# Gate-and-up products of the gated FFNs: weights stationary instead of tokens in 10 of 11 groups

## Chip, cores and metric

One core of a Trainium2 chip runs the whole program in one launch. The metric is device time in microseconds (us), the median of several executions.

## What is computed

256 tokens of width 1024 pass through two blocks in fp32: two layers with two gated FFNs each (around a short convolution in the first, a gated delta rule in the second), then a block with sparse attention, an RWKV-7 mixer and a convolutional FFN. The change concerns the four gated FFNs, with D_FF = 2816:

```python
def swiglu(x, w_gate_up, w_down):
    gate, up = jnp.split(x @ w_gate_up, 2, axis=-1)
    return (jax.nn.silu(gate) * up) @ w_down

for i in range(DEPTH):
    g = norm_g[i]
    ff = swiglu(rms_norm(h, g[0]), ffn_w_gate_up[i, 0], ffn_w_down[i, 0])
    h = h + 0.5 * rms_norm(ff, g[1])
    ...
    ff = swiglu(rms_norm(h, g[4]), ffn_w_gate_up[i, 1], ffn_w_down[i, 1])
    h = h + 0.5 * rms_norm(ff, g[5])
```

## The kernel before

All weights are streamed once from memory, in *groups* of up to 512 output columns, cut in *tiles* of two k-rows (2 x 128 input channels x 512 columns, 256 KB). A gate-and-up group holds 256 gate columns and the 256 up columns that belong to them, with 8 k-rows: four tiles (the very first group has five). An FFN has 11 such groups, then a down product of two groups with 22 k-rows each.

To come near fp32 with the fast fp32r products, each operand is split in a high part (rounded to fp32r) and a low part (the rest). ScalarE writes the high part of a weight tile (`high_to`, L423), VectorE the low part over the raw tile (`low_to`, L433). Both run up to AHEAD = 5 tiles past the last tile of the group in work (`stream_act`, `stream_dve`). There are 6 high buffers and 10 raw ones, so the high part of tile t waits until TensorE has used tile t - 6, the load of tile t for tile t - 10. The tokens' halves are xh and xl, channels on partitions.

TensorE works group by group (`products`, `tile_products`). Tokens are the stationary operand: for each k-row and each of the two token blocks (TB, 128 tokens each) three products of 512 moving weight columns (L458 high by xh, L459 low by xh, L460 high by xl) add up in one PSUM bank per token block. Groups alternate between bank pairs acc0 and acc1. So the output has tokens on partitions: ScalarE takes silu of the gate half, scaled per token by prs (the norm's factor; L700), VectorE multiplies it with the up half and prs (L706) into prod. The down product needs the inner channels on partitions, so TensorE turns prod with four 128x128 transposes into a bank tr (`transpose_prod`, L716), behind the next group's products. ScalarE writes the high part hh (`hidden_high`, L723), VectorE the low part hl (`hidden_low`, L729).

The order on each engine is what `Ffn.pe`, `Ffn.act`, `Ffn.dve` and `Ffn.pool` write down. Banks tr0 and tr1 are handed out in turn as *units*, with the counters tr_ready and tr_free (`free_unit`). `rest_of_vec_pe` and `rest_of_vec_act` (L3715, L3719) turn the other per-channel vectors once, in the first FFN, behind group 0, into the banks aux.

Of the kernel before, what the change touches and what calls it, by code (L numbers as in the profile page):

```python
# [15 lines left out]
ALU = mybir.AluOpType  # L16
# [169 lines left out]
def build(nc, ins, out, stages):  # L186
# [34 lines left out]
    with ctx:  # L221
# [15 lines left out]
        xh = sb("xh", [P, DC, SEQ], F32R)  # L237
        xl = sb("xl", [P, DC, SEQ], F32R)
# [27 lines left out]
        prs = sb("prs", [P, TB])  # L266

# [15 lines left out]
        acc = [[ctx.enter_context(nc.psum_tensor(f"acc{i}{t}", [P, GW], F32)) for t in range(TB)] for i in range(2)]  # L283
        banks = acc[0] + acc[1]
        tr = [ctx.enter_context(nc.psum_tensor(f"tr{i}", [P, GW], F32)) for i in range(2)]
        aux = [ctx.enter_context(nc.psum_tensor(f"aux{i}", [P, GW], F32)) for i in range(2)]
# [7 lines left out]
        acc_free = [sem(f"acc_free{i}") for i in range(2 * TB)]  # L294
# [26 lines left out]
        stored = sem("stored")  # L321

# [18 lines left out]

        place, earlier, count = [], [], [0] * 4
        for gi, g in enumerate(groups):
            if g[0] == "gdn_vz":
# [3 lines left out]
            elif g[0] == "gdn_out":  # L351

                place.append([2 * (gi - first["gdn_out"]) + t for t in range(TB)])
            else:
                low_pair = gi == 0 or 2 in place[-1] or 3 in place[-1]
                place.append([0, 1] if low_pair else [2, 3])
            earlier.append([count[b] for b in place[gi]])
            for b in place[gi]:
                count[b] += 1

# [10 lines left out]
        plan = dict(unit=0, pre=0, post=0, sil=0, hhc=0)  # L371
# [71 lines left out]
        def tile_products(pe, t, tb, xa, xb, before=None):  # L443
# [5 lines left out]
            if k0 == 0 and earlier[gi][tb]:  # L449
                pe.wait_ge(left(gi, tb), earlier[gi][tb])  # L450
            o = at_acc(gi, tb)[:, 0:n]
# [14 lines left out]
        def products(pe, gi, xa, xb, before=None, at_=None, then=None, at2=None, then2=None):  # L466

            for i, t in enumerate(tiles_of[gi]):
# [4 lines left out]
                for tb in range(TB):  # L473
                    tile_products(pe, t, tb, xa, xb, before)

# [131 lines left out]
        def branch_add(dve, s, tb):  # L607
            if s.norm is not None:
                dve.wait_ge(post_sq[tb], 2 * s.norm + 2)
                nc.vector.tensor_scalar(msq[:, tb:tb + 1], ssq[:, tb, 1:2], ssq[:, tb, 0:1], EPS / s.factor ** 2,  # L610
# [108 lines left out]

        def hidden_high(act, g, u):  # L720
# [12 lines left out]
        class Ffn:  # L733
# [3 lines left out]
            def __init__(self, name, g0, vector):  # L737
# [5 lines left out]
                self.unit = plan["unit"] + DC // 2  # L743
                plan["pre"] += 1
                plan["post"] += 1
                plan["unit"] += DC // 2 + FG
                plan["sil"] += 2 * FG
                plan["hhc"] += FG
# [3 lines left out]

            def pe(self, pe, nxt):
                first_products(pe, self)
                if self.n == 0:
                    rest_of_vec_pe(pe)
                for g in range(1, FG):
                    products(pe, self.up + g, xh, xl)
                    transpose_prod(pe, self.up + g - 1, self.unit + g - 1)

                def before(k, tb):
                    u = self.unit + k // 2
# [3106 lines left out]
```

## Time and profile before

| | us |
|---|---|
| median of 3 runs | 1620.4 |
| lowest, highest | 1620.27, 1620.67 |
| span of the profiled execution | 1619.2 |

The span is from the first to the last instruction of the one execution that was profiled; that execution has no time of its own beside it, so it is set against the median of the runs. In the profile, PE is TensorE's matmul, PEld its weight load, DVE VectorE, ACT ScalarE, POOL GpSimd. Durations of matmuls are of pipelined instructions and overlap: the rate is read from their starts.

### The profile page before, as it was taken

What the parts mean: (1) busy time and instruction counts of PE and PEld (TensorE: products, weight loads), DVE (VectorE), ACT (ScalarE), POOL (GpSimd) and SP (SyncE); (2) the same over time, 40 slices, a digit from 0 to 9 for tenths busy, and PEclk for the clock granted to TensorE, in tenths of its full rate; (3) what the DMA queues carried; (4) which work ended last, traced back from release to release, by engine and by line L of the source; (5) the groups of instructions that cost most, each with busy time, mean ns of one, the idle gap of its engine ahead of it and who ended that gap; (6) DMA issues with size and microseconds to landing.
All of it is one profiled execution on the core that took longest, in us unless ns stands there. A gap on an engine that the chain in (4) does not pass through costs nothing.

```text
span 1619.2 us, 25752 instructions
## 1 busy us (share of the span) xinstructions
PE 1601.9 (99%) x10213; PEld 1319.1 (81%) x10213; DVE 1010.7 (62%) x1576; ACT 875.0 (54%) x1358; POOL 135.3 (8%) x153
## 2 busy tenths in 40 slices
PE   8999999999999999999999999999999999999999
PEld 7888888888888888887777788888887787788887
DVE  5555576655556555588766576555667845757673
ACT  6454455654446454596555455544558633566662
POOL 2000001000000000024120000000030200001220
PEclk9999999999999999999999999999999999999999
DMA  8665565666556656553322347655553212556552
GB/s 279 184 186 189 182 202 178 193 184 185 189 183 204 185 184 189 187 161 93 92 79 93 105 150 226 183 184 191 155 172 109 92 29 92 169 177 182 175 182 91
DMA packets 209240, 261.76 MB, mean 162 GB/s; under 512 B 21803, under 2 KB 145122, under 8 KB 209122
## 3 DMA queue, kind: packets, MB, share of 16 engines
q1 hardware_dynamic: 208834, 259.60, 51.8%
q8 instruction: 81, 1.33, 0.3%
q10 hardware_dynamic: 288, 0.52, 0.1%
q14 instruction: 37, 0.30, 0.1%
HBM read 259.01 MB, written 1.05 MB: 161 GB/s over the span
## 4 chain that ended last, share of the span: by engine, by line
PE 90%; DVE 5%; ACT 3%; issue 1%; POOL 0%; DVEq 0%; ACTq 0%
PE acc L458 26%; PE acc L460 25%; PE acc L459 25%; DVE low L433 1%; PE tr L716 1%; PE aux L1003 1%; ACT high L423 1%; PE tr L534 1%; PE tr L3567 1%; PE aux L2774 1%; DVE gdn_cv L1453 1%; PE aux L1011 1%; PE aux L1018 0%; PE acc L3152 0%; PE tr L1889 0%
## 5 line engine op out<-in xcount | busy, mean ns | idle before, releaser
L433 DVE TENSOR_TENSOR low<-raw,high 128x1024 fp32r<-128x1024 f32 (+1 forms) x488 | 588.0, 1221 | 382.7 <-ACT high L423 381.7
L423 ACT ACTIVATE high<-raw 128x1024 fp32r<-128x1024 f32 (+1 forms) x488 | 503.8, 1047 | 348.5 <-PE acc L460 339.0
L458 PE MATMUL acc<-high,xh 128*128 128x512 f32 (+1 forms) x1344 | 538.4, 401 | 3.7 <-DVE low L433 3.0
L460 PE MATMUL acc<-high,xl 128*128 128x512 f32 (+1 forms) x1344 | 521.7, 388 | 0.0
L459 PE MATMUL acc<-low,xh 128*128 128x512 f32 (+1 forms) x1344 | 520.3, 387 | 0.0
L458 PEld LDWEIGHTS acc<-high,xh 128*128 128x128 f32 x1344 | 252.5, 188 | 57.4 <-DVE low L433 5.7
L460 PEld LDWEIGHTS acc<-high,xl 128*128 128x128 f32 x1344 | 252.3, 188 | 53.1
L459 PEld LDWEIGHTS acc<-low,xh 128*128 128x128 f32 x1344 | 253.0, 188 | 46.8 <-issue 0.7
L458 PE MATMUL acc<-high,hh 128*128 128x512 f32 x472 | 185.7, 393 | 0.0
L460 PE MATMUL acc<-high,hl 128*128 128x512 f32 x472 | 183.9, 390 | 0.0
L459 PE MATMUL acc<-low,hh 128*128 128x512 f32 x472 | 183.7, 389 | 0.0
L460 PEld LDWEIGHTS acc<-high,hl 128*128 128x128 f32 x472 | 88.6, 188 | 18.6
L458 PEld LDWEIGHTS acc<-high,hh 128*128 128x128 f32 x472 | 88.7, 188 | 17.7
L459 PEld LDWEIGHTS acc<-low,hh 128*128 128x128 f32 x472 | 88.7, 188 | 17.6
L634 POOL TENSOR_TENSOR rstd<-msq,mhalf 128x1 f32<-128x1 f32 x12 | 6.6, 548 | 753.5 <-DVE msq L610 753.5
L700 ACT ACTIVATE gate_s<-acc,prs 128x256 f32<-128x256 f32 x88 | 41.3, 474 | 44.9 <-PE acc L460 44.9
L706 DVE SCALAR_TENSOR_TENSOR prod<-acc,prs,gate_s 128x256 f32<-128x256 f32 x96 | 45.7, 480 | 19.5 <-ACT gate_s L700 18.1
L543 ACT ACTIVATE xh<-tr,vec 128x128 fp32r<-128x128 f32 x128 | 36.5, 369 | 33.5 <-PE tr L534 33.4
L552 DVE SCALAR_TENSOR_TENSOR xl<-tr,vec,xh 128x128 fp32r<-128x128 f32 x128 | 35.8, 344 | 27.2 <-ACT xh L543 27.2
L3602 DVE SCALAR_TENSOR_TENSOR ffn_conv<-tr,vec,ffn_conv 128x255 f32<-128x255 f32 (+1 forms) x88 | 35.3, 473 | 6.7 <-ACT ffn_conv L3587 6.6
L729 DVE TENSOR_TENSOR hl<-tr,hh 128x512 fp32r<-128x512 f32 x44 | 30.4, 691 | 8.6 <-ACT hh L723 5.6
L593 ACT ACTIVATE prod<-acc 128x512 f32<-128x512 f32 x24 | 14.4, 603 | 33.5 <-PE acc L460 33.5
(471 smaller groups left out, 1644.9 us busy)
## 6 DMA issues: line engine op xcount, KB each, us to landing
raw<-in_ffn_w_gate_up SPq DMA_DIRECT2D x350, 256.0 KB, 3.2
raw<-in_ffn_w_down SPq DMA_DIRECT2D x176, 256.0 KB, 3.0
raw<-in_gdn_w_in SPq DMA_DIRECT2D x96, 256.0 KB, 3.0
raw<-in_ffn_up SPq DMA_DIRECT2D x88, 256.0 KB, 3.2
raw<-in_w_in SPq DMA_DIRECT2D x72, 256.0 KB, 2.9
raw<-in_sc_w_in SPq DMA_DIRECT2D x48, 256.0 KB, 3.1
raw<-in_ffn_down SPq DMA_DIRECT2D x44, 256.0 KB, 2.9
raw<-in_gdn_w_out SPq DMA_DIRECT2D x32, 256.0 KB, 3.0
```

The lines of the kernel that those rows point to most:

```text
L423: nc.scalar.activation(high[t % HIGHS][:, 0:n], raw[t % RAWS][:, 0:n], ACT.Copy).then_inc(high_ready, 1)
L433: nc.vector.tensor_tensor(low[t % RAWS][:, 0:n], raw[t % RAWS][:, 0:n], high[t % HIGHS][:, 0:n].bitcast(F32), ALU.subtract).then_inc(low_r ...
L458: nc.tensor.matmul(o, a, wh, start=(k0 + kk == 0), stop=False)
L459: nc.tensor.matmul(o, a, wl, start=False, stop=False)
L460: mm = nc.tensor.matmul(o, b, wh, start=False, stop=(k0 + kk == k - 1))
L534: mm = nc.tensor.transpose(tr[u % 2][:, i * P:(i + 1) * P], res[:, tb, (4 * h + i) * P:(4 * h + i + 1) * P], ident[:, :])
L543: nc.scalar.activation(xh[:, ch, tb * P:(tb + 1) * P], tr[u % 2][:, i * P:(i + 1) * P], ACT.Copy, scale=s.g0(ch)).then_inc(xh_ready, 1)
L552: x = nc.vector.scalar_tensor_tensor(xl[:, ch, tb * P:(tb + 1) * P], tr[u % 2][:, i * P:(i + 1) * P], s.g0(ch), xh[:, ch, tb * P:(tb + 1) ...
L700: nc.scalar.activation(gate_s[gi % 2][tb][:, :], at_acc(gi, tb)[:, 0:256], ACT.Silu, scale=prs[:, tb:tb + 1]).then_inc(silu_ready, 1)
L706: nc.vector.scalar_tensor_tensor(prod[gi % 2][tb][:, 0:256], at_acc(gi, tb)[:, 256:512], prs[:, tb:tb + 1], gate_s[gi % 2][tb][:, :], ALU. ...
L729: nc.vector.tensor_tensor(fl[:, s], tr[u % 2][:, :], fh[:, s].bitcast(F32), ALU.subtract).then_inc(tr_free[u % 2], 1)
L3602: x = nc.vector.scalar_tensor_tensor(o, tr[u % 2][:, c * SEQ:(c + 1) * SEQ - d], self.weight(tap, h, g, c), o, ALU.mult, ALU.add)
```

## The change

Groups 1 to 10 of each of the four gated FFNs (not of the last, convolutional one) are computed with the *weights* stationary. xh and xl become two planes of one tensor xhl. For each tile, each of four blocks of 128 weight columns (two of gate, two of up) and each k-row there are two products: the high weights with one moving row of 512 columns, xh and xl side by side, and the low weights with the 256 columns of xh, added onto the first 256. The output has inner channels on partitions, with the xl part beside it. Odd groups write acc0 and acc1 as pairs of banks, even ones tr and aux.

ScalarE copies the halves beside (`low_halves_act`), VectorE adds them (`sums_dve`), GpSimd multiplies the gate with rb (the tokens' factors, turned once in each FFN by `factors_pe`), ScalarE takes silu, GpSimd multiplies with up, ScalarE writes hh and VectorE hl. No transposes. The up half is no longer scaled by prs: the norm behind the down product takes that factor out, with its eps scaled in turn (`unscaled_dve`). Group 0 stays as it was but for the up half's scale, and uses the aux banks. Its prod is turned before tile 1 of group 1, the factors before tile 2, and in the first FFN the other vectors before tile 3, now into the banks tr. The gated delta rule's many semaphores for its gates are merged into two counters, with the same waits.

```diff
-        xh = sb("xh", [P, DC, SEQ], F32R)
-        xl = sb("xl", [P, DC, SEQ], F32R)
+        xhl = sb("xhl", [P, 2, DC, SEQ], F32R)
+        xh, xl = xhl[:, 0], xhl[:, 1]
...
+        def turned_products(pe, gi, two, then={}):
+            k = groups[gi][4]
+            for i, t in enumerate(tiles_of[gi]):
+                if i in then:
+                    then[i]()
+                _, k0, kn = tiles[t]
+                pe.wait_ge(low_ready, t + 1)
+                for c in range(4):
+                    o = two[c // 2][:, c % 2, :]
+                    for kk in range(kn):
+                        cols = slice(kk * GW + c * P, kk * GW + (c + 1) * P)
+                        nc.tensor.matmul(o, high[t % HIGHS][:, cols], xhl[:, :, k0 + kk, :], start=(k0 + kk == 0), stop=False)
+                        mm = nc.tensor.matmul(o[:, 0:SEQ], low[t % RAWS][:, cols], xh[:, k0 + kk, :], start=False, stop=(k0 + kk == k - 1))
+                    if k0 + kn == k and c % 2:
+                        mm.then_inc(acc_ready[c // 2], 1)
+                    elif c == 3:
+                        mm.then_inc(used, 1)
...
+            def factors_pe(self, pe):
+                u = self.unit + 1
+                free_unit(pe, u)
+                pe.wait_ge(pre_rstd, TB * (self.n + 1))
+                for tb in range(TB):
+                    mm = nc.tensor.transpose(tr[u % 2][:, tb * P:(tb + 1) * P], prs[:, tb:tb + 1].broadcast_to([P, P]), ident[:, :])
+                mm.then_inc(tr_ready, 1)
+
+            def first_turned_pe(self, pe, g):
+                gi = self.up + g
+                if g == 1:
+                    for b in range(4):
+                        if earlier[gi][b]:
+                            pe.wait_ge(acc_free[b], earlier[gi][b])
+                elif g == 2:
+                    for b in (4, 5):
+                        pe.wait_ge(acc_free[b], earlier[gi][b])
+                    last = self.unit + (1 if self.n else 3)
+                    for u in (last - 1, last):
+                        pe.wait_ge(tr_free[u % 2], u // 2 + 1)
+                if g > 2:
+                    pe.wait_ge(summed, 2 * self.groups_done(g - 2))
+
             def pe(self, pe, nxt):
                 first_products(pe, self)
-                if self.n == 0:
-                    rest_of_vec_pe(pe)
                 for g in range(1, FG):
-                    products(pe, self.up + g, xh, xl)
-                    transpose_prod(pe, self.up + g - 1, self.unit + g - 1)
+                    self.first_turned_pe(pe, g)
+                    then = {}
+                    if g == 1:
+                        then = {1: lambda: transpose_prod(pe, self.up, self.unit), 2: lambda: self.factors_pe(pe)}
+                        if self.n == 0:
+                            then[3] = lambda: rest_of_vec_pe(pe, self.unit + 2)
+                    turned_products(pe, self.up + g, self.two(g), then)
...
-                last = lambda: transpose_prod(pe, self.up + FG - 1, self.unit + FG - 1)
-                last_products(pe, self.out, nxt, hh, hl, before, {2: last})
+                last_products(pe, self.out, nxt, hh, hl, before)
...
+            def low_halves_act(self, act, g):
+                for i, p in enumerate(self.two(g)):
+                    act.wait_ge(acc_ready[i], self.up + g + 1)
+                    nc.scalar.activation(lows[g % 2][:, 2 * i:2 * i + 2, :], p[:, :, SEQ:], ACT.Copy).then_inc(lo_ready, 1)
...
                     stream_act(act, gi)
+                    if g == 0:
+                        silu(act, gi)
+                        continue
+                    if g == 1:
+                        hidden_high(act, 0, self.unit)
+                        self.factors_act(act)
+                        if self.n == 0:
+                            rest_of_vec_act(act, self.unit + 2)
+                    self.low_halves_act(act, g)
+                    high_to(act, ahead + 1)
+                    self.silu_act(act, g)
+                    high_to(act, ahead + 2)
+                    self.high_act(act, g)
...
                     stream_dve(dve, gi)
+                    if g == 1:
+                        hidden_low(dve, 0, self.unit, self.hhc)
+                    self.sums_dve(dve, g)
+                    low_to(dve, ahead + 2)
+                    self.low_dve(dve, g)
...
+            def gate_pool(self, pool, g):
...
+                pool.wait_ge(summed, 2 * n - 1)
+                nc.gpsimd.tensor_tensor(x[:, 0:2, :], x[:, 0:2, :], rb[:, :].unsqueeze(1).broadcast_to([P, 2, SEQ]), ALU.mult).then_inc(gate_scaled, 1)
+                pool.wait_ge(gate_silu, n)
+                pool.wait_ge(summed, 2 * n)
+                nc.gpsimd.tensor_tensor(x[:, 2:4, :], x[:, 2:4, :], x[:, 0:2, :], ALU.mult).then_inc(hidden_ready, 1)
...
-        def rest_of_vec_pe(pe):
+        def rest_of_vec_pe(pe, unit):
             pe.wait_ge(rows_in[1], rows_count(range(1, 5)))
-            for b in range(1, 5):
-                vec_turn(pe, b)
+            for u in (unit, unit + 1):
+                free_unit(pe, u)
+                b = 1 + 2 * (u - unit)
+                vec_turn(pe, tr[u % 2], 0, b)
+                vec_turn(pe, tr[u % 2], P, b + 1).then_inc(tr_ready, 1)
```

TensorE's order, first FFN, end of group 2 and start of group 3, before:

```order
L459 MATMUL acc<-low_51,xh 128x512
L460 MATMUL acc<-high,xl 128x512
L716 MATMUL tr<-ident,prod 128x128 x4
L458 MATMUL acc<-high,xh 128x512
L459 MATMUL acc<-low_52,xh 128x512
L460 MATMUL acc<-high,xl 128x512
```

Now, the front of group 2 behind the last of group 1, with what each waits for:

```order
L522 MATMUL acc<-xhl,low_57 128x256
L521 MATMUL tr<-xhl,high 128x512 [waits tr_free1,tr_free0,low_ready,acc_free5,acc_free4]
L522 MATMUL tr<-xhl,low_58 128x256
L521 MATMUL tr<-xhl,high 128x512
```

Between groups the transposes are gone; group 2 is the first to write the banks tr, and waits for both to be free.

TensorE's order now, first FFN, the front of tile 3 of group 1 (L3872 turns the vectors):

```order
L522 MATMUL acc<-xhl,low_56 128x256
L3872 MATMUL tr<-ident,arena 128x128 [waits tr_free0,rows_in_rest]
L3872 MATMUL tr<-ident,arena 128x128
L3872 MATMUL tr<-ident,arena 128x55 [waits tr_free1]
L3872 MATMUL tr<-ident,arena 128x68
L521 MATMUL acc<-xhl,high 128x512 [waits low_ready]
```

Before, these four stood behind group 0, and wrote aux. Now they wait for a bank that hidden_low frees.

VectorE's order now, first FFN, up to the end of group 1 (L464 is low_to, L790 hidden_low, L922 the sums):

```order
L778 TENSOR_TENSOR prod<-aux,gate_s 128x256 [waits silu_ready] x2
L464 TENSOR_TENSOR low_49<-raw,high 128x1024 [waits high_ready]
L464 TENSOR_TENSOR low_50<-raw,high 128x1024 [waits high_ready]
L464 TENSOR_TENSOR low_51<-raw,high 128x1024 [waits high_ready]
L464 TENSOR_TENSOR low_52<-raw,high 128x1024 [waits high_ready]
L790 TENSOR_TENSOR hl<-tr,hh 128x512 [waits hh_ready]
```

hidden_low stands behind four low parts here, as it did before behind those of the same tiles and two products.

## Rows read from the trace of the kernel before

**Rows 1.** The page: busy time; the chain that ended last, by engine and line
```profile
PE 1601.9 (99%) x10213; PEld 1319.1 (81%) x10213; DVE 1010.7 (62%) x1576; ACT 875.0 (54%) x1358; POOL 135.3 (8%) x153
...
PE 90%; DVE 5%; ACT 3%; issue 1%; POOL 0%; DVEq 0%; ACTq 0%
PE acc L458 26%; PE acc L460 25%; PE acc L459 25%; DVE low L433 1%; PE tr L716 1%; PE aux L1003 1%; ACT high L423 1%; PE tr L534 1%; PE tr L3567 1%; PE aux L2774 1%; DVE gdn_cv L1453 1%; PE aux L1011 1%; PE aux L1018 0%; PE acc L3152 0%; PE tr L1889 0%
```

**Rows 2.** The page, costliest groups: busy us, mean ns, idle before and releaser
```profile
L433 DVE TENSOR_TENSOR low<-raw,high 128x1024 fp32r<-128x1024 f32 (+1 forms) x488 | 588.0, 1221 | 382.7 <-ACT high L423 381.7
L423 ACT ACTIVATE high<-raw 128x1024 fp32r<-128x1024 f32 (+1 forms) x488 | 503.8, 1047 | 348.5 <-PE acc L460 339.0
L458 PE MATMUL acc<-high,xh 128*128 128x512 f32 (+1 forms) x1344 | 538.4, 401 | 3.7 <-DVE low L433 3.0
```

**Rows 3.** Table by stretches, one steady gate-and-up group: us, busy of each engine (instructions), PEclk, DMA
```profile
100.04:111.37 11.33, 11.33 (x53) 9.40 (x52) 6.47 (x7) 5.62 (x8) 0.00 (x0) 1.00 0.63 186
```

**Rows 4.** Timeline of TensorE, a run of 512-column products: start us, us, engine, line
```profile
1168.21 0.39 PE L458 MATMUL acc<-high,xh 128*128 128x512 f32 x1
...
1178.19 0.39 PE L460 MATMUL acc<-high,xl 128*128 128x512 f32 x1
```

**Rows 5.** Timeline of TensorE, around one block of transposes
```profile
59.18 0.39 PE L460 MATMUL acc<-high,xl 128*128 128x512 f32 x1
59.41 0.60 PE L716 MATMUL tr<-ident,prod 128*128 128x128 f32 x4
59.77 0.47 PE L458 MATMUL acc<-high,xh 128*128 128x512 f32 x1
60.08 0.39 PE L459 MATMUL acc<-low,xh 128*128 128x512 f32 x1
...
61.00 0.40 PE L460 MATMUL acc<-high,xl 128*128 128x512 f32 x1
```

**Rows 6.** Timeline of TensorE and its weight loads, narrower groups of 280 and 256 columns
```profile
1178.41 0.29 PE L458 MATMUL acc<-high,xh 128*128 128x280 f32 x1
...
1181.39 0.29 PE L460 MATMUL acc<-high,xl 128*128 128x280 f32 x1
...
1188.09 0.28 PE L458 MATMUL acc<-high,xh 128*128 128x256 f32 x1
1188.09 0.19 PEld L459 LDWEIGHTS acc<-low,xh 128*128 128x128 f32 x1
...
1189.39 0.28 PE L460 MATMUL acc<-high,xl 128*128 128x256 f32 x1
```

**Rows 7.** Timeline of the first FFN: TensorE at the vectors' transposes, VectorE and ScalarE splitting
```profile
24.46 0.79 PE L3715 MATMUL aux<-ident,arena 128*128 128x128 f32 x4
25.70 0.50 PE L458 MATMUL acc<-high,xh 128*128 128x512 f32 x1 [0.46 <-DVE low L433]
...
31.77 4.80 DVE L433 TENSOR_TENSOR low<-raw,high 128x1024 fp32r<-128x1024 f32 x4 [0.79 <-ACT high L423]
...
34.26 1.06 ACT L423 ACTIVATE high<-raw 128x1024 fp32r<-128x1024 f32 x1 [0.62 <-PE acc L460]
```

**Rows 8.** Timeline of ScalarE and VectorE, second FFN, end of group 1 [idle before, releaser]
```profile
314.49 1.06 ACT L423 ACTIVATE high<-raw 128x1024 fp32r<-128x1024 f32 x1 [1.66 <-PE acc L460]
...
315.59 1.23 DVE L433 TENSOR_TENSOR low<-raw,high 128x1024 fp32r<-128x1024 f32 x1 [0.88 <-ACT high L423]
...
317.60 0.60 ACT L723 ACTIVATE hh<-tr 128x512 fp32r<-128x512 f32 x1
...
318.23 0.69 DVE L729 TENSOR_TENSOR hl<-tr,hh 128x512 fp32r<-128x512 f32 x1
```

**Rows 9.** Groups by line and form: busy us, mean ns, idle before
```profile
L604 DVE TENSOR_TENSOR work<-acc,gain 128x512 f32<-128x512 f32 x24 | 16.0, 682 | 1.8 <-ACT prod L593 1.8
...
L593 ACT ACTIVATE prod<-acc 128x512 f32<-128x512 f32 x24 | 14.4, 603 | 33.5 <-PE acc L460 33.5
...
L3617 POOL TENSOR_TENSOR ffn_y<-ffn_conv,ffn_conv 128x512 f32<-128x512 f32 x11 | 14.2, 1288 | 98.8 <-DVE ffn_conv L3602 81.2 <-ACT ffn_conv L3610 17.6
```

More of the change, by code:

```diff
@@ L281, in vcol @@
             return vec[:, at_ + i:at_ + i + 1] if isinstance(i, int) else vec[:, bass.ds(i + at_, 1)]
[L283 to L286, printed above, removed]
+        pairs = [ctx.enter_context(nc.psum_tensor(n, [P, 2, GW], F32)) for n in ("acc0", "acc1", "tr", "aux")]
+        acc0, acc1, tr, aux = ([p[:, i, :] for i in range(2)] for p in pairs)
+        acc = [acc0, acc1]
+        banks = acc0 + acc1 + aux
         landed = [sem(f"landed{i}") for i in range(RAWS)]
@@ L340, in build @@
         y_fm = [arena[:, (DC + 2 * i) * SEQ:(DC + 2 * i + 2) * SEQ] for i in range(2)]
-        place, earlier, count = [], [], [0] * 4
-        for gi, g in enumerate(groups):
-            if g[0] == "gdn_vz":
+        c = Carve(arena_at + 8 * 1024, 18 * 1024)
+        lows = [c(f"lows{i}", [4, SEQ]) for i in range(2)]
+        sums = [c(f"sums{i}", [4, SEQ]) for i in range(2)]
+        rb = c("rb", [SEQ])
+        place, earlier, count = [], [], [0] * 6
+        turned_nth, summed_before, turned_count, on_acc = {}, {}, 0, [0] * 4
+        for gi, g in enumerate(groups):
+            up = g[0] in ("ffn00_up", "ffn01_up", "ffn10_up", "ffn11_up")
+            if up and gi > first[g[0]]:
+                turned_nth[gi] = turned_count
+                turned_count += 1
+                place.append([])
+                if (gi - first[g[0]]) % 2:
+                    on_acc = [turned_count] * 4
+                earlier.append(list(count))
+                continue
+            if up:
+                place.append([4, 5])
+            elif g[0] == "gdn_vz":
                 place.append([0, 1])
@@ L743, in __init__, with two @@
                 self.unit = plan["unit"] + DC // 2
+                self.unscaled = plan["ffn"]
+                plan["ffn"] += 1
                 plan["pre"] += 1
                 plan["post"] += 1
-                plan["unit"] += DC // 2 + FG
-                plan["sil"] += 2 * FG
-                plan["hhc"] += FG
+                plan["unit"] += DC // 2 + (2 if self.n else 4)
+                plan["sil"] += 2
+                plan["hhc"] += 1
+            def two(self, g):
+                return (pairs[0], pairs[1]) if g % 2 else (pairs[2], pairs[3])
@@ L792, in pool @@
             def pool(self, pool, nxt):
+                for g in range(1, FG):
+                    self.gate_pool(pool, g)
                 between_pool(pool, self, nxt)
         class ShortConv:
-            factor, half_first = 1.0, True
+            factor, half_first, unscaled = 1.0, True, None
             def __init__(self):
@@ L1070, in build @@
             NB = KH // 2
-            factor, half_first = 1.0, True
+            factor, half_first, unscaled = 1.0, True, None
             FILL = (13 * (1,),) + 2 * ((2, 1, 1, 1, 1, 1, 1, 1, 1, 1, 1, 2, 1),) + (
```

184 lines of the change are left out of this document (115 added, 69 removed).

## Prediction

> **What bounds it now.** I read the totals and the chain of waits first: TensorE is busy for 1601.9 of 1619.2 us, and the chain that ends last lies 90% on it, three quarters on the three lines of weight products (L458, L459, L460) and 1% on the transposes of L716 [rows 1]. So a change counts by what it does to TensorE's stream, and by what it makes that stream wait for. The groups by line say the same from the other side: VectorE and ScalarE spend their time splitting weights (L433, L423), and each sits idle hundreds of us waiting for the other or for TensorE [rows 2]. Then I read one steady gate-and-up group in the table by stretches: 11.33 us, TensorE busy throughout, VectorE for 6.47, ScalarE 5.62, GpSimd 0, clock 1.00 (the 2.4 GHz level) [rows 3]. There is slack everywhere but on TensorE.
>
> Busy time is no price for a matmul here, since records overlap (0.39 us long, 0.23 apart). The start-to-start distance is. For 512 columns it is 9.98 us over 44 steps, 226.8 ns [rows 4]. The same lines ran with narrower groups: 280 columns, 2.98 us over 23 steps, 129.6 ns; 256 columns, 1.30 us over 11 steps, 118.2 ns; each of these had its own weight load [rows 6]. From 256 to 512 columns that is 0.424 ns per column, which leaves 10 ns (12 from the 280 row) that every matmul costs whatever its width. Four transposes cost, from the last product before them to the second after, 60.08 - 59.18 = 0.90 us against 0.45 for two plain steps: 0.45 us a block, 0.11 each [rows 5].
>
> **The change, part by part.** Four FFNs with 11 groups each are touched; group 0 stays, so 40 groups are turned round.
>
> *Products.* Before: 8 k-rows x 2 token blocks x 3 products = 48 matmuls of 512 columns. Now: 8 x 4 column blocks x (one of 512 columns, one of 256) = 64 matmuls with the same 24576 columns in sum. By the rows: 32 x (226.8 + 118.2) = 11.04 us. The columns are a wash; 16 more matmuls pay 16 x 10 to 12 ns = 0.16 to 0.19 us more than the 48 x 226.8 = 10.89 us of before.
>
> *Transposes of the product.* The block of four behind each turned group goes: 0.45 us. A group took 11.33 us [rows 3] and takes 11.04: 0.29 us less, **11.6 us over 40 groups**.
>
> The row stands against a rule here. The rows show 10 to 12 ns per matmul beside its columns [rows 4, 6]. The Trainium skill (TensorE: Matmul & The Clock Gate, section "Wait — 56ns, not 53.3ns?") gives a fixed cost of about 2.5 ns; by it a group would fall from 10.8 to 10.4 us, 16 us in all instead of 11.6. It already misses the wide matmuls of this trace by 11 ns, so the sum goes by the rows.
>
> *Factors.* The per-token factor must lie along the free axis now, so each FFN turns it with two transposes: 8 x 0.11 = **0.9 us** more on TensorE. The up half is left unscaled and its factor goes into the eps of the next norm, which costs one tiny VectorE operation per FFN.
>
> *Work beside TensorE.* Per group: ScalarE drops two gates of 256 and gains two copies of the low halves and a silu of 512 (four operations of about 0.6 us with the high copy, by the 128x512 rows); VectorE swaps two products of 256 and one subtraction for two sums and one subtraction at about 0.68; GpSimd gains two products at 1.29 [rows 9]. That makes some 6.6 us ScalarE, 6.9 VectorE, 2.6 GpSimd in 11 us: hidden. If this cover were gone, 40 x the overhang would appear. From a group's end the chain low copy, sum, gate product, silu, product, high, low subtraction is under 6 us, and its banks are next written a whole group (11 us) later. The last group's hidden rows are wanted at k = 20 of the down product, 10 tiles on. I cost both at nothing.
>
> *New waits.* Two spots are not covered. ScalarE and VectorE run in order and first split weights up to five tiles ahead; the tile they end on needs a buffer that tile 2 of group 1 gives back. Only behind that stands the turning of group 0's hidden rows (L723, L729), which frees a transpose bank. In the profile: high 1.06 us, then low 1.23, then hl 0.69 [rows 8], 3.0 us from the release.
> - In the first FFN the turning of the remaining per-channel vectors moves from behind group 0 to the front of tile 3 of group 1, into that very bank. The tile it follows has only just been released (the release comes 0.17 us after the next matmul could have started), so TensorE stops 3.1 us. The four transposes (0.45) are paid besides; before, they stood where TensorE then waited 0.46 us for a low part anyway [rows 7], so moving them gains nothing there, and the tiny operation ahead of that low part adds 0.2. Together **3.7 us**.
> - In the three other FFNs group 2 is the first to write the transpose banks. Tile 3 of group 1 (8 x 0.345 = 2.76 us) covers all but 3.0 + 0.17 - 2.76 = 0.4 us, with 0.05 for starting again: 3 x 0.45 = **1.4 us**.
>
> Their ends: nothing, if the splitting runs further behind or ahead than I think, to about twice that, if copies in front are slower. What is queued behind the waiting TensorE is only its own stream, and everything else gains slack from it. DMA issues do not change in number or order.
>
> **Sum:** -11.6 + 0.9 + 3.7 + 1.4 = -5.6 us. Against the profiled span 1619.2 that is 1613.6; the runs' median is 1620.4, 1.2 us above the span, so **1614.8 us**.
>
> **Rivals.**
> 1. *No fixed cost for the narrow matmul* when it follows a wide one (it would start as its columns allow): 10 ns less per pair, at most 12.8 us; at a third of it 1610. The unbroken narrow rows speak against it.
> 2. *The new waits don't appear:* -11.6 + 0.9 = 1609.7. Against: in the profile the same order of ScalarE and VectorE shows in both FFNs [rows 7, 8].
> 3. *The wide matmul is dearer.* Its moving row is in two pieces, 8 KB apart, and ScalarE, VectorE and GpSimd read and write more beside it. Wide steps of 230 ns exist: 60.08 to 61.00 is 0.92 us for 4 [rows 5]. At +4.6 ns on 1280 wide matmuls 5.9 us are lost: 1620.7, no change. At half, 1617.8.
> 4. *Slower: the load shows.* A weight load is recorded at 188 ns [rows 6]. Each wide matmul's weights now load beside a narrow one of 118. If they must be complete before it starts, a pair costs up to 70 ns more: 1280 x 70 = 90 us, 1704 us. It turns the sign from 6.9 ns per pair (8.8 us). Against it: in the narrow rows every load has the same 118 ns and the next starts in time. The Trainium skill (same page, section "LDWEIGHTS (loading the stationary operand)") gives a load of 128 columns 107 ns, which would just fit; the row, not this, sets my chance.
> 5. *It doesn't do what it says:* TensorE waits in every group, for the sums or the hidden chain. 0.2 us in each of 40 groups would be 8 us: 1622.8. Speaks against: the 5 us of slack above.
>
> **Chances.** Forecast 0.58 (own range 1612.5 to 1618); rival 1 0.07; rival 2 0.05; rival 3 0.15; rival 4 0.09; rival 5 0.06. A measurement of this kernel tells 0.2%, 3.2 us, from no change. Faster takes the forecast, rivals 1 and 2: 0.68, with its edge lost 0.67. Same takes rival 3 and that edge: 0.18. Slower takes rival 4 and most of rival 5: 0.15. The range reaches down to both small rivals and up past rivals 3 and 5, 1609 to 1624; beyond it lie the tails of rivals 1 and 4, under 2 in 10.
>
> **What would show it.** In the changed kernel: L716's line with 32 transposes instead of 192; 1280 matmuls of 128x256 beside 1280 wide ones; pairs of 345 ns start to start; a steady group of 11.04 us without idle time; one TensorE stop of about 3 us near 35 us, before the vectors' transposes, put down to VectorE's hl; three of 0.4 us at the starts of group 2; VectorE's low still waiting for ScalarE's high. It is wrong if pairs take over 350 ns, if a group shows regular waits, or if the 3 us stop is absent.

## The result, and the profile after

| | before | changed |
|---|---|---|
| median | 1620.41 us (4 runs) | **1639.48 us** (4 runs) |
| lowest, highest | 1620.27, 1620.67 | 1639.11, 1639.81 |
| profiled span | 1619.2 | 1637.4 |
| mean granted clock of that execution | 1.00 | 0.995 |

The ratio is 1.0116, 95% interval 1.0102 to 1.0129: the change makes the kernel slower by 19 us, 1.2%. The prediction said 1614.8 and faster, with a range up to 1624: wrong in sign and in range.

The page of the changed kernel, busy time and the chain that ended last, against [rows 1]:

```profile
PE 1605.7 (98%) x10701; PEld 1339.3 (82%) x10701; DVE 1025.5 (63%) x1580; ACT 914.0 (56%) x1402; POOL 253.5 (15%) x233
...
PE 88%; DVE 6%; ACT 3%; issue 1%; POOL 0%; DVEq 0%; ACTq 0%
```

The span grew by 18.2 us and TensorE's busy time by only 3.8, so 14.4 us of the loss is time in which TensorE stands. Its share of the chain fell from 90 to 88%, and VectorE's rose from 5 to 6%. The waits of TensorE, from the trace (in all, times, longest, us):

```profile
PE tr L771 <- DVE prod L778: 8.9, 4, 2.3
PE tr L3872 <- DVE hl L790: 3.2, 1, 3.2
...
PE tr L521 <- issue: 1.3, 3, 0.5
```

The first row wasn't forecast at all: four stops of 2.2 us, one in each gated FFN, before the transposes of group 0's product (L771). The second is the stop before the vectors' transposes that I put at 3.1, the third the three stops at the front of group 2 that I put at 0.4 each. 13.4 us in all.

Here is one of the first kind, in the second FFN: ScalarE, VectorE, then TensorE (start, duration, engine, line, what it does; idle before it and its releaser in brackets).

```profile
314.90 3.91 ACT L454 ACTIVATE high<-raw 128x1024 fp32r<-128x1024 f32 x4 [0.85 <-POOL prs L633]
318.71 0.81 ACT L755 ACTIVATE gate_s<-aux,prs 128x256 f32<-128x256 f32 x2
...
315.99 4.63 DVE L464 TENSOR_TENSOR low<-raw,high 128x1024 fp32r<-128x1024 f32 x4 [0.92 <-ACT high L454]
320.54 0.74 DVE L778 TENSOR_TENSOR prod<-aux,gate_s 128x256 f32<-128x256 f32 x2
...
318.92 0.28 PE L522 MATMUL acc<-xhl,low 128*128 128x256 f32 x1
321.43 0.63 PE L771 MATMUL tr<-ident,prod 128*128 128x128 f32 x4 [2.23 <-DVE prod L778]
```

The product (L778) wants silu (L755), and both stand in their engine's order behind four splitting tiles (L454, L464), which start only once the norm's factor prs is there, at 314.90 (both engines wait for it, `rms_known`, at the top of their program for an FFN). The product is done at 320.54 + 0.74 = 321.28. Group 1's first tile ended with the product that starts at 318.92, so TensorE stands from 319.20 to 321.43.

The same rows of the kernel before, which I had not read, show the order was already so (the same work stands 10.2 us earlier in that trace):

```profile
304.72 3.91 ACT L423 ACTIVATE high<-raw 128x1024 fp32r<-128x1024 f32 x4 [0.85 <-POOL prs L581]
308.53 0.81 ACT L700 ACTIVATE gate_s<-acc,prs 128x256 f32<-128x256 f32 x2
...
305.88 4.63 DVE L433 TENSOR_TENSOR low<-raw,high 128x1024 fp32r<-128x1024 f32 x4 [1.82 <-ACT high L423]
306.07 0.39 PE L458 MATMUL acc<-high,xh 128*128 128x512 f32 x1
310.43 0.87 DVE L706 SCALAR_TENSOR_TENSOR prod<-acc,prs,gate_s 128x256 f32<-128x256 f32 x2
...
316.96 0.60 PE L716 MATMUL tr<-ident,prod 128*128 128x128 f32 x4
```

There the product was done at 311.30 and its transposes came at 316.96, behind all of group 1 (which starts at 306.07), with 5.7 us to spare. The change moves that block to the front of tile 1, three tiles earlier, ahead of the product.

The first of the four stops leaves a second mark. Timeline of TensorE in the first FFN:

```profile
27.51 0.40 PE L521 MATMUL acc<-xhl,high 128*128 128x512 f32 x1
...
27.87 0.40 PE L521 MATMUL acc<-xhl,high 128*128 128x512 f32 x1
...
30.94 1.08 PE L771 MATMUL tr<-ident,prod 128*128 128x128 f32 x4 [2.21 <-DVE prod L778]
...
32.47 0.63 PE L521 MATMUL acc<-xhl,high 128*128 128x512 f32 x1
...
33.11 0.63 PE L521 MATMUL acc<-xhl,high 128*128 128x512 f32 x1
```

Before the stop a pair (wide and narrow) takes 27.87 - 27.51 = 0.36 us, behind it 33.11 - 32.47 = 0.64. The table by stretches (length, busy time of each engine with its instructions, PEclk, DMA share, GB/s) gives the reason:

```profile
31.00:34.00 3.00, 3.00 (x11) 2.71 (x12) 2.36 (x2) 1.16 (x2) 0.00 (x0) 0.50 1.10 360
42.00:48.00 6.00, 5.94 (x19) 4.86 (x20) 0.69 (x1) 1.38 (x5) 0.53 (x1) 0.51 0.00 2
48.00:60.00 12.00, 12.00 (x69) 10.41 (x69) 6.79 (x7) 6.82 (x9) 2.69 (x3) 1.00 0.57 176
314.00:332.00 18.00, 15.32 (x86) 12.94 (x85) 12.09 (x15) 11.29 (x16) 0.96 (x2) 1.00 0.73 229
509.00:512.00 3.00, 3.00 (x11) 2.71 (x12) 2.08 (x2) 0.00 (x0) 0.00 (x0) 0.50 0.81 282
```

From 31 to 34 us and from 42 to 48 the granted clock is 0.50 and 0.51, the 1.2 GHz level; between them (35 to 38) and from 48 on it is 1.00. TensorE had stood for 2.2 us before the first of these stretches and for 3.2 before the second. The third FFN shows the same behind its 2.2 us stop (509 to 512), and so does the fourth; the second, whose stop is as long, keeps 1.00 (314 to 332). From the start of group 1 to that of group 2, read from TensorE's timeline, the four FFNs take 22.52, 14.83, 16.40 and 16.41 us.

A steady group in the table by stretches, against [rows 3]:

```profile
100.04:111.37 11.33, 11.33 (x66) 9.82 (x65) 6.80 (x7) 6.61 (x9) 2.99 (x2) 1.00 0.61 187
```

One of the page's costliest groups, against [rows 2]:

```profile
L521 PE MATMUL acc<-xhl,high 128*128 128x512 f32 x640 | 232.0, 405 | 1.0 <-DVE low L464 1.0
```

Groups by line and form, GpSimd's second product in a turned group and the weight loads of the narrow matmuls that write tr, against [rows 6, 9] (busy us, mean ns, idle before):

```profile
L957 POOL TENSOR_TENSOR sums<-sums 128x512 f32<-128x512 f32 x40 | 66.1, 1651 | 30.7 <-ACT sums L881 30.7
...
L522 PEld LDWEIGHTS tr<-xhl,low 128*128 128x128 f32 x320 | 60.3, 188 | 0.0
```

The splitting is unchanged (1224 ns a tile against 1221), and TensorE has 640 wide products of this form on the bank acc, as many on the others. Beside TensorE the sizing was right: VectorE 6.80 us in a group (forecast 6.9), ScalarE 6.61 (6.6), GpSimd 2.99 (2.6; its second product takes 1.65 us, not 1.29). The weight loads of the narrow matmuls are recorded at 188 ns (L522; those on acc, half-clock stretches among them, at 193 on average), and cost nothing that shows.

But the steady group does not take 11.04 us. GpSimd's product with rb (L954) starts once in every turned group, so its starts give the groups' length. First FFN, then second:

```profile
59.88 1.30 POOL L954 TENSOR_TENSOR sums<-sums,rb 128x512 f32<-128x512 f32 x1 [7.56 <-DVE sums L922]
...
71.19 1.30 POOL L954 TENSOR_TENSOR sums<-sums,rb 128x512 f32<-128x512 f32 x1 [7.58 <-DVE sums L922]
...
342.71 1.30 POOL L954 TENSOR_TENSOR sums<-sums,rb 128x512 f32<-128x512 f32 x1 [7.58 <-DVE sums L922]
...
353.81 1.31 POOL L954 TENSOR_TENSOR sums<-sums,rb 128x512 f32<-128x512 f32 x1 [7.41 <-DVE sums L922]
```

11.31 us in the first FFN, 11.10 in the second, each through all the steady groups of its FFN. The third is like the second, the fourth like the first. Before, a group took 11.35 us from one block of L716 to the next; the 11.33 of the prediction is the length of the window in [rows 3].

TensorE's starts show that these are two different cycles of steps. In the first FFN the wide steps run 232, 241, 236 ns and the narrow ones 118, 120, 113, over and over: three pairs in 1060 ns. In the second the wide steps are 231 and 233, the narrow ones 112 and 117: two pairs in 693 ns.

### The profile page after: what moved, and what is told of

Same layout as the page of the kernel before. It is cut to its first block, busy times and chain, and to the rows that moved or that the text cites. A ratio compares the mean times of both kernels' runs of the same rounds, so it can differ in the third digit from the quotient of the medians.

```text
span 1637.4 us, 26918 instructions
## 1 busy us (share of the span) xinstructions
PE 1605.7 (98%) x10701; PEld 1339.3 (82%) x10701; DVE 1025.5 (63%) x1580; ACT 914.0 (56%) x1402; POOL 253.5 (15%) x233
## 4 chain that ended last, share of the span: by engine, by line
PE 88%; DVE 6%; ACT 3%; issue 1%; POOL 0%; DVEq 0%; ACTq 0%
PE acc L491 16%; PE acc L493 16%; PE acc L492 16%; PE acc L521 9%; PE tr L521 5%; PE aux L521 5%; PE acc L522 4%; DVE low L464 3%; PE aux L522 2%; PE tr L522 2%; ACT high L454 1%; PE aux L1172 1%; PE tr L586 1%; PE tr L3724 1%; PE aux L2931 1%
## 5 line engine op out<-in xcount | busy, mean ns | idle before, releaser
L464 DVE TENSOR_TENSOR low<-raw,high 128x1024 fp32r<-128x1024 f32 (+1 forms) x488 | 589.9, 1224 | 387.2 <-ACT high L454 386.5
L454 ACT ACTIVATE high<-raw 128x1024 fp32r<-128x1024 f32 (+1 forms) x488 | 504.1, 1048 | 327.0 <-PE acc L493 169.2
L491 PE MATMUL acc<-high,xhl 128*128 128x512 f32 (+2 forms) x640 | 259.8, 406 | 1.2 <-DVE low L464 0.5
L493 PE MATMUL acc<-high,xhl 128*128 128x512 f32 (+2 forms) x640 | 247.3, 386 | 0.0
L492 PE MATMUL acc<-low,xhl 128*128 128x512 f32 (+2 forms) x640 | 246.4, 385 | 0.0
L521 PE MATMUL acc<-xhl,high 128*128 128x512 f32 x640 | 232.0, 405 | 1.0 <-DVE low L464 1.0
L522 PE MATMUL acc<-xhl,low 128*128 128x256 f32 x640 | 181.1, 283 | 0.0
L521 PEld LDWEIGHTS acc<-xhl,high 128*128 128x128 f32 x640 | 123.3, 193 | 30.9 <-DVE low L464 1.4
L491 PEld LDWEIGHTS acc<-high,xhl 128*128 128x128 f32 x640 | 120.3, 188 | 27.6 <-issue 4.5
L493 PEld LDWEIGHTS acc<-high,xhl 128*128 128x128 f32 x640 | 120.2, 188 | 25.1
L492 PEld LDWEIGHTS acc<-low,xhl 128*128 128x128 f32 x640 | 120.6, 188 | 20.9 <-issue 0.7
L522 PEld LDWEIGHTS acc<-xhl,low 128*128 128x128 f32 x640 | 123.6, 193 | 0.1
L521 PE MATMUL tr<-xhl,high 128*128 128x512 f32 x320 | 115.8, 397 | 1.3 <-issue 1.3
L521 PE MATMUL aux<-xhl,high 128*128 128x512 f32 x320 | 115.6, 396 | 0.0
L954 POOL TENSOR_TENSOR sums<-sums,rb 128x512 f32<-128x512 f32 x40 | 52.0, 1301 | 347.9 <-DVE sums L922 347.9
L522 PE MATMUL aux<-xhl,low 128*128 128x256 f32 x320 | 89.3, 279 | 0.0
```

The costliest lines, as they stand in the source:

```text
L454: nc.scalar.activation(high[t % HIGHS][:, 0:n], raw[t % RAWS][:, 0:n], ACT.Copy).then_inc(high_ready, 1)
L464: nc.vector.tensor_tensor(low[t % RAWS][:, 0:n], raw[t % RAWS][:, 0:n], high[t % HIGHS][:, 0:n].bitcast(F32), ALU.subtract).then_inc(low_r ...
L491: nc.tensor.matmul(o, a, wh, start=(k0 + kk == 0), stop=False)
L492: nc.tensor.matmul(o, a, wl, start=False, stop=False)
L493: mm = nc.tensor.matmul(o, b, wh, start=False, stop=(k0 + kk == k - 1))
L521: nc.tensor.matmul(o, high[t % HIGHS][:, cols], xhl[:, :, k0 + kk, :], start=(k0 + kk == 0), stop=False)
```

## The experiments

Theories at the outset: the time is in the stops and in the clock that they cost (letter A in the expectations; letter B is its rival in each case); or it is in the pairs of wide and narrow products, either because the moving row lies in two pieces (rival 3, letter C in the expectations) or because the widths alternate (letter E). The kernel before ran beside each set (medians 1620.67 to 1620.89).

**The changed kernel again, unaltered**

> The changed kernel once more, unaltered. Its trace showed turned groups of 11.30 us in the first and the last of the four FFNs and 11.09 us in the two between. If that belongs to the program, the same FFNs show the same values (within 0.02 us). If it is a state that an execution falls into, they come out otherwise. Both theories expect a time of about 1639.5 us and a stop of 2.2 us before the transposes of the product in each FFN.

1639.04 us, span 1637.3. Starts of the same product in the same two FFNs:

```profile
59.29 1.30 POOL L954 TENSOR_TENSOR sums<-sums,rb 128x512 f32<-128x512 f32 x1 [7.41 <-DVE sums L922]
...
70.39 1.31 POOL L954 TENSOR_TENSOR sums<-sums,rb 128x512 f32<-128x512 f32 x1 [7.41 <-DVE sums L922]
...
353.36 1.31 POOL L954 TENSOR_TENSOR sums<-sums,rb 128x512 f32<-128x512 f32 x1 [7.57 <-DVE sums L922]
...
364.68 1.29 POOL L954 TENSOR_TENSOR sums<-sums,rb 128x512 f32<-128x512 f32 x1 [7.58 <-DVE sums L922]
```

Table by stretches:

```profile
42.00:48.00 6.00, 6.00 (x22) 4.84 (x21) 0.69 (x1) 1.47 (x6) 0.89 (x1) 0.55 0.00 2
320.00:323.00 3.00, 3.00 (x13) 2.52 (x12) 1.17 (x2) 0.00 (x0) 0.00 (x0) 0.58 0.59 207
510.50:513.50 3.00, 3.00 (x21) 2.65 (x20) 1.64 (x2) 0.00 (x0) 0.00 (x0) 1.00 0.66 223
```

Now the first FFN has groups of 11.10 us and the second 11.32: the other way round. The third and the fourth are at 11.31 too. And now it is the second FFN whose clock falls behind its stop (0.58, 320 to 323), while the third keeps 1.00 (510.5 to 513.5), with a stop of 2.22 us that ends at 510.0; the fourth keeps it too. So neither is fixed by the place in the program: both which rate an FFN takes and which 2.2 us stop drops the clock change between executions of the same kernel. The stops themselves do not change: 8.9, 3.2 and 1.4 us. The Trainium skill (TensorE: Matmul & The Clock Gate, section "What's actually happening") says that the gate watches activity in windows that run freely, not tied to the program; equal stops that drop the clock in one execution and not in another agree with it, but no run here isolates it.

**Clock kept through the stops.** TensorE gets something to do while it waits: 10 and 14 products of 128 columns that nobody reads (`keep_clock`). What it waits for comes no sooner.

```
 def kept():
     free_unit(pe, self.unit)
+    keep_clock(pe, 10, tr[self.unit % 2])
     transpose_prod(pe, self.up, self.unit)
 def kept_vec():
+    keep_clock(pe, 14, aux[0])
     rest_of_vec_pe(pe, self.unit + 2)
```

> Dummy products fill the two kinds of long stop: 10 before the transposes of the product in each FFN, 14 before the vectors' transposes in the first. Theory A: the stops themselves cost 2.2 us x 4 and 3.2 us, and what comes on top is TensorE's clock, which the trace shows at 0.5 for some 16 us behind three of the four stops; with the array busy through them the clock stays at 1.0 and about 7 us come back: about 1632 us. Theory B: the slow stretches behind the stops are starved of weights, not clocked down; then the time stays at 1639 to 1640 us and pairs of 640 ns remain behind the stops.

1634.05 us, span 1632.3. Table by stretches:

```profile
27.00:34.00 7.00, 7.00 (x50) 6.34 (x49) 6.42 (x7) 5.40 (x7) 0.00 (x0) 1.00 1.08 362
38.00:46.00 8.00, 7.96 (x56) 7.04 (x55) 3.21 (x4) 4.41 (x11) 1.30 (x1) 1.00 0.27 74
```

The clock stays at 1.00, the pairs of 0.64 us are gone, and 5 us come back. The forecast was 7, from the execution that had lost in three FFNs. The four lengths from group 1 to group 2 are now 18.36, 14.83, 14.83, 14.83; against these the first execution lost 4.2 + 0 + 1.6 + 1.6 = 7.3 us to the clock, the repeated one (22.4, 16.42, 14.83, 14.84) 5.6. That the span fell by only 5.1 from the first execution is the two rates: here one FFN ran at 11.10 (the first) where there two had, 1.9 us in groups 2 to 10. The clock's part is shown; the rest of the loss stays, so it isn't the clock alone.

**Everything turned later.** The factors are turned at tile 1 of group 1; group 0's product at tile 1 of group 3, with its high and low parts ahead of that group's splitting; the vectors in halves, in groups 1 and 3. Same arithmetic, same matmuls.

```
-then = {1: lambda: transpose_prod(pe, self.up, self.unit), 2: lambda: self.factors_pe(pe)}
-    then[3] = lambda: rest_of_vec_pe(pe, self.unit + 2)
+then = {1: lambda: self.factors_pe(pe)}
+    then[2] = lambda: rest_of_vec_pe(pe, self.unit + 1, 0)
...
+if g == 3:
+    def turn_first():
+        pe.wait_ge(summed, 2 * self.groups_done(2))
+        transpose_prod(pe, self.up, self.turned_unit)
+        if self.n == 0:
+            rest_of_vec_pe(pe, self.unit + 3, 1)
+    then = {1: turn_first}
```

> The computation is the same; the transposes of group 0's product move from tile 1 of group 1 to tile 1 of group 3, those of the vectors to groups 1 and 3, and ScalarE and VectorE turn group 0's hidden rows ahead of their splitting for group 3. Theory A: all stops (8.9 + 3.2 + 1.3 us) and the clock's loss (7 us) vanish: 1639.5 - 20.4 = about 1619 us, with turned groups still at 11.1 to 11.3 us. Theory B (the products themselves are what costs, the stops only move): 1630 us or more, with new waits of 2 us in group 3 or 4.

1619.37 us (10 runs, 1618.29 to 1621.41), span 1617.8, clock 1.00; ratio to the kernel before 0.9993, interval 0.9984 to 1.0003. Its TensorE waits:

```profile
PE aux L491 <- DVE low L464: 3.0, 4, 1.2
PE aux L573 <- POOL minus L3944: 1.9, 1, 1.9
```

All three kinds of stop are gone; what leads the list now are waits at other products for a low part of the weights (3.0 us, as much as VectorE's low is charged with in [rows 2]) and for a row that GpSimd prepares, and both stood there before. 20.1 us come back: 13.4 of stops and 5.6 to 7.3 of clock are 19.0 to 20.7. In the spans it is 19.6, though only one FFN is at the short rate here and two were in the changed kernel's first execution. Read from TensorE's starts, 23.8 us come back between group 1 and group 2, where the stops were (the four lengths together are 25.1 us above the kernel before in the changed one, 1.2 here), and groups 2 to 10 take 4.2 more, the moved blocks and the rate. That settles where the loss is. It also leaves a kernel that is no faster than before, where the sum had 11.6 us of gain from the groups. So the second error is in the groups.

**Moving row in one piece.** The halves of a k-row side by side in memory.

```
-xhl = sb("xhl", [P, 2, DC, SEQ], F32R)
+xhl = sb("xhl", [P, DC, 2, SEQ], F32R)
```

> Only the layout of the tokens' high and low planes changes, so that the 512 moving columns lie in one piece instead of two that are 8 KB apart. Theory C: the two pieces make the wide product dear (233 to 237 ns against 226.8 before); then its step falls to about 227 ns, groups to 11.0 us, and the time by 4 to 10 us to 1630 to 1635 us. Theory D: the layout has no part in it; steps of 233 to 237 ns and 1639.5 us stay.

1639.63 us, span 1637.9, groups of 11.31 us in three FFNs and of 11.09 in one: no effect. Rival 3's two pieces fall.

**Which rate, once more.** The kernel with everything turned later, a second time:

> The version with the late transposes once more, for a second trace. Its first one had groups of 11.09 us in the first FFN and 11.31 in the three others. Theory E (the alternation of widths can settle at either of two rates, by chance): another FFN or another number of them is fast, and each FFN that changes sides moves the time by 7 to 8 x 0.21 = some 1.6 us. Theory G (the place in the program decides): the same three are slow and the time is within 0.5 us of 1619.4.

1620.62 us, span 1618.9. GpSimd's starts in the first FFN, first execution and second:

```profile
72.45 1.30 POOL L967 TENSOR_TENSOR sums<-sums,rb 128x512 f32<-128x512 f32 x1 [7.41 <-DVE sums L935]
...
83.55 1.30 POOL L967 TENSOR_TENSOR sums<-sums,rb 128x512 f32<-128x512 f32 x1 [7.41 <-DVE sums L935]
```

and

```profile
72.20 1.29 POOL L967 TENSOR_TENSOR sums<-sums,rb 128x512 f32<-128x512 f32 x1 [7.58 <-DVE sums L935]
...
83.50 1.30 POOL L967 TENSOR_TENSOR sums<-sums,rb 128x512 f32<-128x512 f32 x1 [7.57 <-DVE sums L935]
```

The steady groups of the first FFN took 11.10 us in the one and 11.30 in the other, of the same program; the other three FFNs 11.31 in both. The span is 1.1 us longer: from group 1 to the end of group 10 the first FFN takes 1.6 us more, and the second execution had reached group 1 0.6 us sooner. It would explain that this kernel's runs spread over 3.1 us where those of before spread over 0.4 to 1.3.

The rate is not a property of a whole FFN. In the first execution TensorE's starts have group 2 of the first FFN at 11.31 us (37.53 to 48.84), and only behind the transposes in group 3 do the groups fall to 11.10. In the traces of the kernels with alternating widths it changes only behind a stop or a block of transposes, never inside the unbroken stretch that follows. Nor is it all chance: the eight pairs of tile 0 of group 1 ran at 353 ns in all 24 FFNs of the six executions profiled.

**Order of the widths.** Both start from the kernel with everything turned later. In one the eight wide products of a tile come first, then its eight narrow ones. In the other, in each column block, two wide, then two narrow:

```
 for kk in range(kn):
     cols = slice(kk * GW + c * P, kk * GW + (c + 1) * P)
     nc.tensor.matmul(o, high[t % HIGHS][:, cols], xhl[:, :, k0 + kk, :], start=(k0 + kk == 0), stop=False)
+for kk in range(kn):
+    cols = slice(kk * GW + c * P, kk * GW + (c + 1) * P)
     mm = nc.tensor.matmul(o[:, 0:SEQ], low[t % RAWS][:, cols], xh[:, k0 + kk, :], start=False, stop=(k0 + kk == k - 1))
```

> On top of the version with the late transposes, each tile does its 8 wide products first and then its 8 narrow ones, instead of wide and narrow in turn. Theory E: the alternation itself makes the wide step fall into one of two values (about 230 or 237 ns, groups of 11.09 or 11.31 us, one of them for a whole FFN and not the same one in each execution); in runs of one width the steps are 226.8 and 118.2 ns, groups 11.04 to 11.10 us in all four FFNs, and the time 1619.4 - 6 = about 1613 us. Theory F: the 11.31 us are a state that any turned group can be in, whatever the order; then some FFNs stay at 11.3 us and the time at 1618 to 1620 us.

1615.54 us (6 runs, 1615.29 to 1616.21), ratio 0.9968, interval 0.9956 to 0.9980.

> The same with two wide and then two narrow products for each column block: half as many changes of width. Theory E: the surcharge per change halves, slow groups of 11.2 us, fast ones of 11.06, about 1616 us. Theory F: groups of 11.09 and 11.31 us as before, 1619 us.

1614.59 us (4 runs, 1614.20 to 1615.30), ratio 0.9962, interval 0.9949 to 0.9976: **faster than the kernel before by 6.1 us and than the changed one by 24.9.** Timeline of TensorE in a steady group, order two and two (start, length of the run of instructions, its count at the end):

```profile
351.62 0.63 PE L521 MATMUL acc<-xhl,high 128*128 128x512 f32 x2
...
355.10 0.63 PE L521 MATMUL acc<-xhl,high 128*128 128x512 f32 x2
```

The same with eight and eight; the line at 354.82 is the sixth of the eight, taken out of their run by a narrower window:

```profile
353.66 2.00 PE L520 MATMUL acc<-xhl,high 128*128 128x512 f32 x8
...
354.82 0.62 PE L520 MATMUL acc<-xhl,high 128*128 128x512 f32 x2
...
355.50 1.11 PE L525 MATMUL acc<-xhl,low 128*128 128x256 f32 x8
356.45 2.00 PE L520 MATMUL acc<-xhl,high 128*128 128x512 f32 x8
```

GpSimd's starts in the first FFN with two and two:

```profile
60.43 1.30 POOL L969 TENSOR_TENSOR sums<-sums,rb 128x512 f32<-128x512 f32 x1 [8.38 <-DVE sums L937]
...
71.58 1.30 POOL L969 TENSOR_TENSOR sums<-sums,rb 128x512 f32<-128x512 f32 x1 [7.45 <-DVE sums L937]
```

Two pairs lie between the starts of two wide runs, ten between 351.62 and 355.10. A pair takes 3.48 / 10 = 348 ns, a group 11.15 us, and it does so in all four FFNs and in every execution looked at; with eight and eight 11.17. The long rate of 11.31 is gone with the alternation, as letter E had it. Its sizes did not come out: the two-and-two pairs don't reach the 345 ns of the rows before. In the eight-and-eight order the wide step is (355.50 - 353.66) / 8 = 230 ns and the narrow one (356.45 - 355.50) / 8 = 119, against 226.8 and 118.2 before.

That 230 is no even step. The first five take (354.82 - 353.66) / 5 = 232 ns, the last three (355.50 - 354.82) / 3 = 227, the step of the plain rows. The kernel before has the same behind its transposes: from 60.08 us six steps take 1.38 us, 230 each, and the next three 0.68, 227 each, in its timeline of TensorE, which goes on from [rows 5]:

```profile
61.46 0.39 PE L459 MATMUL acc<-low,xh 128*128 128x512 f32 x1
...
62.14 0.39 PE L459 MATMUL acc<-low,xh 128*128 128x512 f32 x1
```

So some five wide steps behind narrower products are dear, whatever the kernel, and then the step is the old one. In the two-and-two and in the alternating order no wide step gets that far.

**Both orders, with the row in one piece**

> The best version so far (late transposes, two wide then two narrow products; groups of 11.15 us in all four FFNs, 1614.6 us) with the tokens' high and low columns in one piece. Its wide step is some 230 ns where plain wide products took 226.8. If the two pieces cost these 3 ns, groups fall to 11.04 us and the time by 4 us to about 1610.5 us; if they do not, 11.15 us and 1614.6 us stay.

1614.72 us (5 runs, 1614.43 to 1615.13), ratio 0.9962, interval 0.9949 to 0.9976; groups 11.15.

> The same layout with runs of 8 wide and 8 narrow products (groups of 11.17 us with two pieces). If the two pieces cost something, the runs of wide products show it most plainly: 226.8 ns instead of 230 to 232 within a run, groups of 11.06 us. If not, 11.17 us.

1615.75 us, groups 11.17. The two pieces cost nothing in this order either. Why the first wide steps behind narrower ones are dear stays open.

**Two and two, with the transposes where the change put them**

> The changed kernel with two wide and two narrow products in turn, and the transposes where the change put them. If order and stops are two separate matters, the groups fall to 11.15 us and the time by 30 x 0.16 or so, to about 1635 to 1637 us, with the stops of 2.2 and 3.2 us and a clock below 1 unchanged. If the order took part in the stops, they are shorter.

1634.28 us, span 1632.6, clock 0.997; groups 11.15, the stops unchanged (9.0 us in four, 3.2 in one). It is one run, 5 us faster than the changed kernel, and not all of that is the order. Groups 2 to 10 give 1.9 us against the changed kernel's first execution, 3.8 against the repeated one, which had one FFN fewer at the short rate. The rest lies between group 1 and group 2, where the clock happened to fall behind other stops (lengths 19.88, 16.33, 16.39, 14.85). The order heals none of the stops: two separate matters.

## Why the prediction was wrong, step by step

The 18.2 us of span, by TensorE's starts in the two traces: from the start of group 1 to that of group 2 the four FFNs take 70.2 us together, before 45.1, which is +25.1. Groups 2 to 10 take 5.1 less. The rest of the program takes 1.8 less, about what the block of group 10 in the down product cost (4 x 0.45). That is all of it.

Of the 25.1, the stops are 13.4, the clock 7.3, the factors 0.9 and the vectors' transposes and small work 0.65 (both as forecast, not measured apart). Starting again is an estimate: a stop is counted from the end of a record of 0.28 us, where the next start was due after 0.12, so each of the eight costs 0.16 more, 1.3 us. The 1.5 us left are about what 32 pairs of 346.6 to 353.4 ns take more than the 48 products of before (0.2 to 0.4 in each FFN).

The forecast of -5.6 is thus off by 23.8 us: 8.9 for stops that it did not have, 7.3 for the clock that it did not have, 6.2 for the products (-5.4 where it had -11.6), and 1.4 for the rest, most of it what starting again costs.

- **"Two spots are not covered."** This step failed: there is a third spot, the turning of group 0's product, which the sum had at nothing. With the clock behind it, it set the sign. Of the two things that were moved ahead, group 0's transposes and the vectors', I followed only the second back to its producers. For the first I asked what it frees (the bank) and not when its input is ready. The trace of before had the answer: product done at 311.30, group 1 begun at 306.07, and one tile of 2.76 us: TensorE there at 308.8, a stop of 2.5 us. Measured 2.23, four times: 8.9 us. (The other remedy, silu and product ahead of the splitting, was not tried.)
- **Vectors' stop, 3.1 us:** 3.16 measured. **Fronts of group 2, 3 x 0.4:** 1.3 measured. The chain of high, low and hl was sized rightly; rival 2 falls.
- **What a stop costs beyond itself.** Not in the sum at all. Behind the stops the clock fell to the 1.2 GHz level in three of four FFNs in the profiled execution and in two in the repeated one: 7.3 and 5.6 us. The forecast stop of 3.1 us alone should have raised the question; it is part of the 4.2 us lost in the first FFN.
- **Products, 32 x (226.8 + 118.2) = 11.04 us.** A term mis-sized: 11.10 or 11.31, pairs of 346.6 or 353.4 ns. Gain over before 0.25 us a group at the one rate, 0.04 at the other, where 0.29 was forecast. Steps measured in unbroken rows of one width did not carry over to alternating ones. This error alone takes the whole forecast gain: 5.6 us over 1280 pairs are 4.4 ns a pair, and they were 5.0 ns dearer on average. (The 6.9 ns that the prediction gives for a turned sign, under rival 4, are the 8.8 us to a measurable loss.) Pair over 350 ns stood among the marks of a wrong prediction, and half the FFNs show it.
- **Rival 1** (narrow ones without fixed cost) falls: 119 ns in rows of eight. **Rival 3** had about the size of the products' error (+5.0 ns a pair on average against its +4.6), by another mechanism: the three kernels with the row in one piece exclude the two pieces. Its 230 ns steps of [rows 5] are the dear ones behind a block of narrower products. The reads and writes beside TensorE, its other ground, were not varied; the same steps in the kernel before, without that work, speak against them. **Rival 4** falls: loads of 188 ns beside narrow matmuls, and no rate above 353.4 ns a pair at clock 1.00.
- **Rival 5** had the right kind (TensorE waits for late work), but in the wrong place: not in the steady groups, which have no wait at all, but once in each FFN, where the look-ahead splitting starts late.
- **Work beside TensorE at nothing:** right [rows 9]. **Factors and the eps operation:** nothing in the stages contradicts them, but no run measured them apart.

The mechanism meant to save time is real: with the stops moved away and the widths in twos, 40 groups at 11.15 instead of 11.35 give 7.9 us, less 0.9 for the factors 7.0, and the span shows 1619.2 - 1612.5 = 6.7. Of these, 0.65 lie ahead of group 1 of the first FFN (reached at 25.05 us, before at 25.70), where executions of one kernel differ as much.

## What to carry to other kernels

When a step moves ahead in the order of one engine, look in the trace for the end of everything it reads, and for what stands before that producer on its own engine; a late start of in-order look-ahead work (here behind prs) makes a product late by many times its own duration. Price a stop of TensorE with the clock that may fall behind it (here 0 to 1.6 us behind 2.2, and 4.2 behind 2.2 and 3.2 together), and move the step to where its input has long been ready. A step measured among its like is not the step of a mixed sequence: try the order in twos before judging a split into wide and narrow matmuls. And before explaining a difference of a few us between single runs, divide both traces at the same starts: here 2 us and more went with which rate and which clock an execution had drawn.

## What was not expected of the hardware

- Alternating 512- and 256-column products ran at one of two rates, 346.6 or 353.4 ns a pair, at the same granted clock of 1.00, each a fixed cycle of two or three pairs, and the same program took one or the other in different executions. It changed only behind an interruption. In twos it was 348 ns always. What sets the rate is open.
- A stop of 2.2 us dropped the granted clock in some executions and FFNs and not in others. The stop of 3.2 us dropped it in both executions of the changed kernel that were profiled (0.51 and 0.55 from 42 to 48 us). With the row in one piece and with the widths in twos, transposes as in the change, it was alike: in these four executions the clock fell behind 10 of 16 stops of 2.2 us and behind all four of 3.2.
- Behind narrower products some five wide steps take 232 ns on average before the step is 227 again, with the moving row in one piece or two, in the kernel before as in the changed ones. Why is open.
